# A new order for the chunk-attention and state-space phase of a two-layer encoder kernel

## The reference, cut to what matters

```
a_r = mag*cos(li*dt); a_i = mag*sin(li*dt)           # 32 groups, 64 states each
bbar = f(a, lam) * b                                  # the input matrices
x[t] = a * x[t-1] + bbar @ u[t]                       # associative scan over 512 frames
y = gelu(Re(C x) + D u);  ob = y * sigmoid(y @ glu_w + glu_b)
oa = softmax(q k^T / 8 + bias[relative distance], masked to the band) @ v
h = layer_norm(alpha*h + concat(oa, ob) @ even_w_out)
```

## Time and profile before

| | us |
|---|---|
| median of 3 runs | 1328.69 |
| the profiled execution, own time | 1320.62 |
| its span on the core | 1318.9 |
| PE busy | 1215.8 |
| ACT / DVE / POOL busy | 422.8 / 438.6 / 550.5 |

### The profile page before, as it was taken

One profiled execution on the slowest core, in us unless ns is written; L12 is line 12 of the kernel. 1 busy time (PEld: TensorE's weight loads), 2 busy tenths in 40 slices (PEclk: granted clock), 3 DMA queues, 4 the chain that ended last, 5 costly groups with the idle time before them and its releaser, 6 DMA issues.

```text
span 1318.9 us, 14982 instructions
## 1 busy us (share of the span) xinstructions
PE 1215.8 (92%) x6191; PEld 985.3 (75%) x6191; DVE 438.6 (33%) x743; ACT 422.8 (32%) x571; POOL 550.5 (42%) x279
## 2 busy tenths in 40 slices
PE   6956687799999999999999899989799999999997
PEld 5745465588888888888877677767698888888885
DVE  6974356425111111100160577773711111110005
ACT  5313224623322222211232455452332222222121
POOL 5765242045544444444355322212544444444442
PEclk9978898899999999999999999999899999999999
DMA  6702213233433333332333212211243333333321
GB/s 169 196 20 58 50 42 105 96 97 96 116 100 99 100 97 96 95 97 96 96 96 112 80 33 64 65 32 41 78 122 96 97 97 99 99 101 101 96 64 64
DMA packets 152499, 117.31 MB, mean 89 GB/s; under 512 B 18672, under 2 KB 138520, under 8 KB 152432
## 3 DMA queue, kind: packets, MB, share of 16 engines
q1 hardware_dynamic: 152432, 116.36, 29.9%
HBM read 112.00 MB, written 3.17 MB: 87 GB/s over the span
## 4 chain that ended last, share of the span: by engine, by line
PE 82%; DVE 9%; ACT 3%; POOL 2%; issue 2%; DMA 1%; SPq 0%; DVEq 0%; ACTq 0%
PE ps L1363 16%; PE ps L1364 15%; PE ps L1365 15%; PE ps L1385 8%; PE ps L1386 8%; PE ps L1387 8%; DVE sg L923 2%; PE ps L1734 1%; PE ps L1758 1%; DVE ps L923 1%; POOL wlo L512 1%; PE ps L1745 1%; PE ps L1497 1%; POOL h L585 1%; PE ps L1592 1%
## 5 line engine op out<-in xcount | busy, mean ns | idle before, releaser
L512 POOL TENSOR_TENSOR wlo<-raw,whi 128x1024 fp32r<-128x1024 f32 x190 | 459.2, 2421 | 654.9 <-ACT whi L617 654.4
L1363 PE MATMUL ps<-xhi,whi 128*128 128x512 f32 (+1 forms) x992 | 383.1, 386 | 11.3 <-POOL wlo L512 5.1
L1364 PE MATMUL ps<-xlo,whi 128*128 128x512 f32 (+1 forms) x992 | 376.7, 380 | 0.0
L1365 PE MATMUL ps<-xhi,wlo 128*128 128x512 f32 (+1 forms) x992 | 376.3, 379 | 0.0
L617 ACT CAST whi<-raw 128x1024 fp32r<-128x1024 f32 x190 | 201.3, 1066 | 265.7 <-PE ps L1387 187.9
L1363 PEld LDWEIGHTS ps<-xhi,whi 128*128 128x128 f32 x992 | 189.6, 191 | 56.0 <-issue 7.5
L1365 PEld LDWEIGHTS ps<-xhi,wlo 128*128 128x128 f32 x992 | 189.5, 191 | 34.9
L1364 PEld LDWEIGHTS ps<-xlo,whi 128*128 128x128 f32 x992 | 190.0, 192 | 32.6
L923 DVE TENSOR_TENSOR gt<-ps,sg 128x512 f32<-128x512 f32 x44 | 30.4, 692 | 372.7 <-PE ps L1365 372.7
L1385 PE MATMUL ps<-whi,ghi 128*128 128x512 f32 x352 | 137.2, 390 | 0.0
L1387 PE MATMUL ps<-whi,glo 128*128 128x512 f32 x352 | 137.1, 389 | 0.0
(11 more groups left out here) (206 smaller groups left out, 1140.7 us busy)
## 6 DMA issues: line engine op xcount, KB each, us to landing
raw<-in_ffn_w SPq DMA_DIRECT2D x132, 512.0 KB, 3.7
raw<-in_odd_w_in SPq DMA_DIRECT2D x24, 512.0 KB, 3.8
raw<-in_even_w_in SPq DMA_DIRECT2D x16, 512.0 KB, 4.8
h<-in_x SPq DMA_DIRECT2D x8, 512.0 KB, 5.7
raw<-in_even_w_out SPq DMA_DIRECT2D x8, 512.0 KB, 3.8
raw<-in_odd_w_out SPq DMA_DIRECT2D x8, 512.0 KB, 3.6
bias<-rel_scratch SPq DMA_DIRECT2D x8, 256.0 KB, 5.0
out<-h SPq DMA_DIRECT2D x4, 512.0 KB, 2.6
```

The costliest lines, as they stand in the source:

```text
L512: eng.tensor_tensor(lo, raw_of(b), hi, ALU.subtract).then_inc(w_lo, 1)
L1363: eng.matmul(o_, w_hi_, x_hi_, start=start, stop=False)
L1364: eng.matmul(o_, w_hi_, x_lo_, start=False, stop=False)
L1365: return eng.matmul(o_, w_lo_, x_hi_, start=False, stop=stop)
```

## The change: what it does

1. **Phase table.** The repeated squaring on DVE goes. The angles come from two PE products (`pl` rows 5 and 6 by a ramp 0 to 63, `angles` and `turns`, four matmuls of 512 columns), DVE takes off whole turns in five passes over 128x1024, and ACT takes two sines of 128x1024. `phases_ready` now comes from ACT. Many small DVE operands move from SBUF to PSUM (`scratch`, `pwp`, `wide`).
2. **Order of the state-space steps.** `SSM_AT` is replaced by four tables; the kernels of a group (s = 3, 4) come ahead of its states (s = 2 before, or a tick later), and steps that waited for a read right before them now have other work between. Copies of `gk` and the filling of `decay` move from DVE to ACT.
3. **SP queue.** The `b` tables are loaded later and weight blocks earlier; `rel_scratch` is stored after the `u` stores; block 16 (`weights_upto(17)`) stands ahead of `load_u(3)`.
4. **Ticks.** The scores are negated, so that the row minimum serves as the exponent's bias as it is and one small DVE instruction per piece goes. GELU runs after ticks 5 and 8, and the first two gate products in ticks 9 and 10; the last two follow `pair_product(3)`.
5. **LayerNorm.** Tiles 0 to 2 are finished like tile 3: nine instructions of the form L1252 in the first three norms and three in the last come to DVE, and twelve ACT and twelve POOL instructions over 128x1024 go.

```diff
-        SSM_AT = {-1: ((0, 6), (1, 0), (1, 1)), 0: ((1, 2), (1, 3), (1, 4)), 2: ((1, 5), (2, 0), (2, 1)),
-                  3: ((1, 6), (2, 2), (2, 3), (2, 4)), 4: ((3, 0), (3, 1)), 5: ((2, 5), (3, 2), (3, 3), (3, 4)),
-                  6: ((2, 6),), 7: ((3, 5),), 8: ((3, 6),)}
-        ROTATE_AT = {1: 1, 4: 2, 6: 3}
-        SSM_ORDER = [(0, st) for st in range(STEPS - 1)] + [step for n in sorted(SSM_AT) for step in SSM_AT[n]]
+        SSM_BANK = (5, 7)
+
+
+        SSM_FIRST = ((1, 0), (1, 1))
+        SSM_BEFORE = {2: ((2, 0), (2, 1)), 5: ((3, 2),)}
+        SSM_AT = {-1: ((0, 5),), 0: ((0, 6), (1, 2)), 1: ((1, 3), (1, 4)), 2: ((2, 2),), 3: ((1, 5),),
+                  4: ((1, 6), (3, 0), (3, 1)), 5: ((2, 5),), 6: ((2, 6),), 7: ((3, 5),), 8: ((3, 6),)}
+        SSM_AFTER = {3: ((2, 3), (2, 4)), 5: ((3, 3), (3, 4))}
+        SCAN_AT = {0: 1, 2: 2, 5: 3}
+        SSM_ORDER = [(0, st) for st in (0, 1, 3, 4, 2)] + list(SSM_FIRST)
+        SSM_ORDER += [step for n in sorted(SSM_AT) for at_ in (SSM_BEFORE, SSM_AT, SSM_AFTER) for step in at_.get(n, ())]
...
+        angles, turns = psf[:, 0:PAIRS * NC], psf[:, PAIRS * NC:2 * PAIRS * NC]
...
                 eng.dma_start(h[:, t, :], xt[t]).then_inc(x_landed[t], 16)
-            weights_upto(2)
-            eng.dma_start(bnr[:], b_re[0].rearrange("(a b) p i -> (b p) a i", b=2)).then_inc(b_landed, 16)
-            eng.dma_start(bni[:], b_im[0].rearrange("(a b) p i -> (b p) a i", b=2)).then_inc(b_landed, 16)
+            weights_upto(3)
...
-            weights_upto(5)
+            eng.dma_start(bnr[:], b_re[0].rearrange("(a b) p i -> (b p) a i", b=2)).then_inc(b_landed, 16)
+            weights_upto(4)
+            eng.dma_start(bni[:], b_im[0].rearrange("(a b) p i -> (b p) a i", b=2)).then_inc(b_landed, 16)
+            weights_upto(6)
...
-            eng.dma_start(rel_dram, relext[:]).then_inc(rel_stored, 16)
-            weights_upto(6)
             store_u(0)
             weights_upto(7)
             load_u(0)
             store_u(1)
             weights_upto(8)
-            load_u(1)
             store_u(2)
             weights_upto(9)
+            load_u(1)
             store_u(3)
+            sp_.wait_ge(relext_ready, 2)
+            eng.dma_start(rel_dram, relext[:]).then_inc(rel_stored, 16)
+            weights_upto(10)
             sp_.wait_ge(rel_stored, 16)
             load_bias(0)
-            load_bias(1)
             weights_upto(13)
             load_toep(0)
+            load_bias(1)
             weights_upto(14)
             load_u(2)
             weights_upto(16)
             load_toep(1)
+            weights_upto(17)
+            load_bias(2)
             load_u(3)
-            load_bias(2)
-            weights_upto(17)
+            weights_upto(18)
             load_toep(2)
-            weights_upto(18)
             load_bias(3)
+            weights_upto(20)
             load_toep(3)
             weights_upto(21)
...
-                    eng.tensor_tensor(h[:, t, :], h[:, t, :], lnp[:, 1, :], ALU.add).then_inc(h_ready, 1)
+                lower_upto(f + 2)
 
...
+            act.wait_ge(x_ready, NT)
+            eng.activation(pl[:, 4, :], pl[:, 9, :], ACT.Exp, scale=float(L)).then_inc(mag_ready, 1)
+            eng.activation(scratch(MAG_), pl[:, 9, :], ACT.Exp).then_inc(mag_ready, 1)
             act.wait_ge(arg_ready, 1)
-            eng.activation(pl[:, 6, :], pl[:, 12, :], ACT.Sin).then_inc(trig_ready, 1)
-            eng.activation(pl[:, 5, :], pl[:, 13, :], ACT.Sin).then_inc(trig_ready, 1)
+            eng.activation(pl[:, 16, :], pl[:, 12, :], ACT.Sin).then_inc(trig_ready, 1)
+            eng.activation(pl[:, 17, :], pl[:, 13, :], ACT.Sin).then_inc(trig_ready, 1)
...
+            act.wait_ge(angle_ready, 1)
+            eng.activation(phi[:].rearrange("p a c -> p (a c)"), whole[:], ACT.Sin).then_inc(phases_ready, 1)
+            eng.activation(phr[:].rearrange("p a c -> p (a c)"), turns, ACT.Sin, bias=half_pi[:]).then_inc(phases_ready, 1)
+            for q in range(1, AT):
                 upper_upto(q + 4)
                 project_out(q, None)
...
             def softmax_exp(n):
                 w = PIECE_W[n % 3]
-                act.wait_ge(s_negmax, n + 1)
+                act.wait_ge(s_biased, segments_upto(n + 1))
...
+            UPPER_AT = {-1: 13, 0: 14, 1: 15, 2: 16, 3: 17, 5: 18, 6: 19, 8: 20}
...
+                if n in SCAN_AT:
...
+                if n == 5:
+                    y_gate(0)
+                    y_gate(1)
                 if n == 8:
+                    y_gate(2)
+                    y_gate(3)
+                    for q in range(AT):
+                        y_upper(q)
...
-                    act.wait_ge(rstd_ready, (NT - 1) * n + t + 1)
-                    eng.mul(h[:, t, :], h[:, t, :], lns[:, t, 2:3]).then_inc(scaled, 1)
...
+            link(less(q_(TH8), q_(T), TWO_PI_REST, q_(TH8)))
+            eng.tensor_scalar(q_(TURN8), q_(TH8), 1 / (2 * math.pi), None, ALU.mult).then_inc(ramp_ready, 1)
+            dve.wait_ge(marks_ready, 1)
+            eng.tensor_tensor_scan(ramp[:], marks[:], marks[:], 0.0, ALU.mult, ALU.add).then_inc(ramp_ready, 1)
             for t in range(NT):
                 lower_x(0, t)
...
+            dve.wait_ge(angle_done, 1)
+            link(eng.tensor_scalar(whole[:], turns, ROUNDER, ROUNDER, ALU.add, ALU.subtract))
+            link(less(angles, whole[:], TWO_PI_1, angles))
+            link(less(angles, whole[:], TWO_PI_REST, angles))
...
+            link(eng.tensor_scalar(whole[:], angles, PI_BELOW, -PI_BELOW, ALU.min, ALU.max))
+            eng.scalar_tensor_tensor(out=turns, in0=whole[:], scalar=-1.0, in1=angles, op0=ALU.mult,
+                                     op1=ALU.min).then_inc(angle_ready, 1)
...
+                by_i = pw[:, 1, :, n:n + 1].broadcast_to((P, PAIRS, n))
+                cmul(pwp[:, 0, :, n + 1:2 * n + 1], pwp[:, 1, :, n + 1:2 * n + 1], pwp[:, 0, :, 1:n + 1],
+                     pwp[:, 1, :, 1:n + 1], by_r, by_i, PAIRS * n, (PAIRS, n))
...
                         col += 1
-                dve.wait_ge(s_biased, segments_upto(n + 1))
-                eng.tensor_scalar(sm[:, n % 2, 1, 0:col], sm[:, n % 2, 0, 0:col], -1.0, None,
-                                  ALU.mult).then_inc(s_negmax, 1)
...
-                    rotate(ROTATE_AT[n], 1)
+                ssm_vector(SSM_BEFORE.get(n, ()))
+                if n - 1 in SCAN_AT:
+                    rotate(SCAN_AT[n - 1], 1)
                 if n + 1 < A_PIECES:
                     normalised(n + 1)
-                if n in ROTATE_AT:
-                    rotate(ROTATE_AT[n], 2)
+                if n - 1 in SCAN_AT:
+                    rotate(SCAN_AT[n - 1], 2)
                 ssm_vector(SSM_AT.get(n, ()))
+                ssm_vector(SSM_AFTER.get(n, ()))
                 if n == 8:
+                    dve.wait_ge(*ssm_made(AT - 1, 2))
+                    for q in range(AT):
+                        y_lower(q)
+                if n == 9:
                     pair_lower(0)
...
                     dve.wait_ge(std_ready, NT * n + t + 1)
-                    if t < NT - 1:
-                        eng.reciprocal(lns[:, t, 2:3], lns[:, t, 1:2]).then_inc(rstd_ready, 1)
-                    else:
-                        link(eng.reciprocal(lns[:, t, 2:3], lns[:, t, 1:2]))
-                        eng.scalar_tensor_tensor(out=h[:, t, :], in0=h[:, t, :], scalar=lns[:, t, 2:3],
-                                                 in1=lnp[:, 1, :], op0=ALU.mult, op1=ALU.add).then_inc(h_last, 1)
+                    link(eng.reciprocal(lns[:, t, 2:3], lns[:, t, 1:2]))
+                    eng.scalar_tensor_tensor(out=h[:, t, :], in0=h[:, t, :], scalar=lns[:, t, 2:3],
+                                             in1=lnp[:, 1, :], op0=ALU.mult, op1=ALU.add).then_inc(
+                                                 h_ready if t < NT - 1 else h_last, 1)
...
                 turn(0, t)
+            pe.wait_ge(ramp_ready, 2)
+            pe.wait_ge(x_ready, 2)
+            for row, into in ((5, angles), (6, turns)):
+                for half in range(2):
+                    c = slice(half * S, (half + 1) * S)
+                    mm = eng.matmul(into[:, c], pl[:, row, :], ramp[:, c], start=True, stop=True)
+            mm.then_inc(angle_done, 1)
             pe.wait_ge(x_ready, NT)
...
             pe.wait_ge(pl_ready, 1)
-            for i in range(7):
+            for i in range(5):
                 mm = eng.transpose(ps[:, 6, i * PAIRS:(i + 1) * PAIRS], pl[:, i, :], ident[0:PAIRS, 0:PAIRS])
             mm.then_inc(pl_turned, 1)
+            project(2, 2)
             pe.wait_ge(c_landed, 64)
-            for src, bank in ((cdr, 7), (cdi, 0)):
+            pe.wait_ge(phases_ready, 2)
...
                                        ident[:])
             mm.then_inc(c_turned, 1)
-            project(2, 2)
...
+            def glu(m):
+                b = GLU + m // 2
+                pe.wait_ge(w_lo, b + 1)
```

(14 more changed lines are left out.)

349 lines of the change are left out of this document (175 added, 174 removed).

## The result

The changed kernel takes 1250.74 us (median of 4 runs, 1249.41 to 1250.93) where the kernel before, measured beside it, took 1327.95 (4 runs, 1322.28 to 1330.81): a ratio of 0.942, 95% interval 0.939 to 0.945. The forecast was 1277 with 1257 to 1300, a gain of 52 us; it is 77. The profiled execution went from 1320.62 to 1250.77, by 69.9 us.

What follows compares the result with a forecast made beforehand. PE's work and holes were taken to bound the kernel. Holes gave 16.6 + 24.4 + 6.8 = 47.8 us, less 4 reserve, plus 7 clock and 1 norms: 52 off 1328.7, so 1277 us, range 1257 to 1300.

Steps and rivals of the forecast that it cites:

- Stage by stage: PE holes in three stretches before the output projection: 18.3, 27.2 and 13.1 us fall to 1.7, 2.8 and 6.3, gaining 47.8.
- The waits named: PE waits expected to stay: 1.8, 0.6, 0.3 and 0.1 us in the ticks; 1.7, 3.0 and 1.6 in the tail.
- The angle products: Four new PE matmuls for the phase table, in the first stretch: put at 1.1 us of added work.
- The reserve of 4: 4 us taken off the gain from holes, for delays that a walk without queues misses.
- The clock: Slow PE work up to the output projection: 7 us back, between 0 and 15, of at most 15.5.
- The start stays slow, and the last ticks keep holes: I take half back: Step pricing the clock up to the output projection: half of at most 15.5 us of slow work comes back, 7 us.
- LayerNorm: New finish of tiles 0 to 2 in the norms: about 1 us gained, between 6 gained and 8 lost.
- norms lose: Rival: POOL's subtraction slows nine new DVE instructions in the first three norms, perhaps 8 us on PE, 1285; within forecast's 70%.
- The other signs: Up to the output projection: phases_ready before 35, first scores at 82 to 84, clock above 0.9; norms without POOL wait.
- Half of it: Rival: a hole of the ticks comes back at another place, so the gain is 32 us, 1297; chance 17%.
- The table's slack: Phase table before the first scores: it must be 40 us late to matter as today.
- slower: Rival: short matmuls leave the clock down up to the output projection; slower by over 0.3% from 36% on, 3% chance.

Runs made afterwards that it cites:

- e1: Changed kernel with the old LayerNorm finish (ACT's multiplication, POOL's addition) for tiles 0 to 2: 1258.86 us.
- e15: Changed kernel with PE waiting before the first scores for an otherwise unneeded transfer of 6144 single elements, a hole of 12.87 us: 1266.59 us.
- e16: Changed kernel with PE waiting before the first scores for an otherwise unneeded transfer of 12288 single elements, a hole of 26.16 us: 1278.19 us.
- e8: Changed kernel with steps (q, 3) straight behind (q, 2) again for quarters 1 to 3, and (3, 2) back behind (2, 5): 1262.24 us.
- e2: Kernel before with only the new LayerNorm finish: 1316.32 us against 1323.58 of before, ratio 0.9939.
- e3: Changed kernel with POOL waiting for tile 2's result before the second weight split behind a norm: 1249.38 us.
- e6: Kernel before without the phase table's doubling loop, its values left at 1 and 0: 1313.05 us against 1325.19, ratio 0.9919.
- e10: Changed kernel with the angle products behind the first projection, ramp scan behind the xlo subtractions, range reduction behind the small table: 1255.23 us.
- e13: e10 with the angle products over 128 rows, 112 of them zero, in place of 16: 1252.05 us.
- e12: e10 with POOL's weight splits behind a norm held until tile 2 is ready, from the fourth on until tile 3 is: 1252.76 us.

## Why the prediction was wrong

The mechanism and the holes were right; the sizes of other terms were not, above all those of the clock and of the norms. By the prediction's own sum, in traces of one profiled execution each:

- **Stage by stage.** Left were to be 1.7, 2.8 and 6.3 us. Left are 0, 4.56 and 4.47, and in front of them 4.75 of angle products less 2.3 of holes that these fill at the start. From 0 to the output projection holes fell from 68.3 to 16.4 us, 51.9; less 4.75 of new work 47.1, where the sum had 47.8. The waits named came at 1.74 (said 1.8, before (2, 2)), 0.78 (0.6, before (3, 3)), 0.94 (0.3) and 0.46 (0.1), in the tail 1.89 for the first `ylo` (1.7) and 1.39 for piece 10 (3.0).
- **The angle products** were mis-sized: put at 1.1 by the mean of the last stretch, they took 4.75, since each runs as two recorded matmuls, of 0.59 us on the mean (4.75 by 8); where the clock stayed at 1.00, in e1, they took 3.67, still over three times the term. The first projection came 1.9 later, not 0.6. It was hidden in the good agreement above, because the `uP` wait and the rest of the first stretch went away wholly.
- **The reserve of 4** for what a walk misses wasn't needed. DVE was held up (one product of the first rotation takes 2.44 us at 74.55, the next ones 0.95 to 1.09), but no wait of PE comes of it.
- **The clock**, +7.4. Busy time to the output projection fell from 189.9 to 180.2 although 4.75 were added: 14.4 of slow work went, nearly all of the 15.5 that the prediction gave as the bound. The step that failed is "The start stays slow, and the last ticks keep holes: I take half back". The start did stay slow (0.76 in the 4.68 us from 14.00 on, 0.50 in the next 4.42) and 4.47 us of holes stayed in the last stretch, but the level was 1.00 from the first scores to the last quarter. A long hole cost 2 to 3 us of slow work at either length, a short one about 1.2 (e15, e16; 3.7 by three in e8), so what counts is how many go, and of before's dozen all but small ones went.
- **LayerNorm**, +7.4. Put at 1, measured 8.4 in the traces, 8.1 in e1, 7.3 in e2. The step that failed is the one that priced a norm at its one visible wait of 2.19 less 1.4 of later `xlo`. In the first norm two smaller waits (0.35 and 0.21) and 2.24 us of clock behind the three go with it, and the later `xlo` costs 0.7. The third norm, for which the sum has no term, gives 1.3. The 0.6 of the last norm was right (0.5). The rival "norms lose" had its mechanism (3.26 instead of 1.28 where POOL reads beside DVE) but in one of the nine new instructions: 2 us of wait, 2.5 of time (e3).
- **Median against profile.** 52 plus 4, less 0.7, plus 7.4 of clock and 7.4 of norms is 70, the 69.9 of the traces. The other 7 of the 77 are before's own scatter: its profiled execution was 7.3 below its median, the changed kernel's on its own. In all its runs before took from 1318.8 to 1330.8 us with a clock of 0.956 to 0.966 (1319.54 at 0.966, 1328.21 at 0.959 side by side), with medians from 1322.2 to 1328. Taking the median of before less a gain measured in one trace carried this in.

The output projection, said to start near 205, started at 196.6. The other signs stood: `phases_ready` at 30.3, first scores at 82.24, no wait for `zin_i`, clock over 0.9, no POOL wait in the norms but a longer one for `xlo`. "Half of it" needed a wait to come back in the ticks, and none did; in e6, where only one part is made, one of 4.7 us comes, ahead of the ticks. The table's slack, said to be 40 us, was tried at 10.7. One sum of the "slower" rival is off: 52 us and 4 more are a third of its 168, not 36%.

## What to carry over

Price a hole as its length plus a piece of 1 to 3 us for the slow work behind it (an estimate from e8, e15, e16 and the 14.4 us by before's dozen), so that closing many short ones is worth more than their sum; and price a wait together with the small ones after it on the same path. When one hole of a chain is closed, look for the one that was hidden under it (4.7 us of `toep` in e6): a part made alone gave less than its hole. Before you move work out of a kernel's start, look whether it fills a hole there (2.36 us in e10). The kernel with the holes scattered more here (1318.8 to 1330.8) than the one without (1249.4 to 1253.1), so compare medians with medians and traces with traces.

## What was not expected of the hardware

Four gapless products over 16 rows were followed by 3 us at 1.2 GHz (granted 0.50), and the same products padded with zeros to 128 rows by none (1.00); padding made the kernel 3.2 us faster in e13 against e10. e12 has the slow piece as e10 has it. What in the chip makes the difference is not shown, and the start is not settled by this alone: in e1 it ran at 1.00 with the 16-row products too.

A hole of 26.16 us cost no more slow work behind it than one of 12.87 (1.97 and 2.75 us, one trace each).
